# A hybrid decoder layer on one core: three sums of weights and one difference of token operands go from VectorE to GpSimd, and one token tile is scaled by itself

## The reference

```
h    = rms_norm(x, g_pre)                       # x: 512 x 2048
proj = h @ w_in                                 # q, k, v, gate of each group; forget gates
A: 6 heads, MoBA block-sparse causal attention, T5 relative bias
B: 6 heads, forgetting attention: log_sigmoid(fb + b_forget), cumulative sum as bias
C: 4 heads, attention into rms_norm(mem, g_mem) @ w_mem_kv   # mem: 256 x 2048
y    = concat(out_group * silu(gate))
x    = x + rms_norm(y @ w_out, g_post)
```

## Time and profile before

| | |
|---|---|
| median of 3 runs | 887.97 us (887.89 to 888.15) |
| profiled execution, whole | 889.66 us |
| its span | 887.9 us |
| TensorE busy | 865.6 us, 97% |
| VectorE busy | 727.2 us, 82% |
| ScalarE busy | 536.8 us, 60% |
| GpSimd busy | 75.9 us, 9% |
| mean granted TensorE clock | 0.994 of full |

### The profile page before, as it was taken

The page is one execution under the profiler, slowest core; times in us unless marked ns, Lnnn a source line. Parts: engine busy times, 40 slices in busy tenths (PEclk is TensorE's granted clock), DMA queues, the critical chain, the costliest instruction groups (busy, mean ns, idle before and its releaser), DMA issues.

```text
span 887.9 us, 13757 instructions
## 1 busy us (share of the span) xinstructions
PE 865.6 (97%) x5181; PEld 766.0 (86%) x5181; DVE 727.2 (82%) x1025; ACT 536.8 (60%) x918; POOL 75.9 (9%) x84
## 2 busy tenths in 40 slices
PE   9998999999999999999999999999999989999995
PEld 6997999988888888888888888888888878778884
DVE  5799789988888888888888888888888886975558
ACT  6795556565656565656565656565656575654452
POOL 0000310000000000000030303030301000000000
PEclk9999999999999999999999999999999999999999
DMA  9980586567668577657677768577644597466845
GB/s 289 303 200 23 165 181 165 148 172 159 160 171 196 137 178 176 161 163 177 153 183 170 165 171 185 144 185 170 161 121 107 172 366 259 146 214 208 289 190 189
DMA packets 179143, 161.37 MB, mean 182 GB/s; under 512 B 7353, under 2 KB 144217, under 8 KB 177670
## 3 DMA queue, kind: packets, MB, share of 16 engines
q1 hardware_dynamic: 170166, 142.66, 52.6%
q0 software_dynamic: 8704, 16.78, 13.7%
q10 hardware_dynamic: 208, 1.07, 0.4%
HBM read 152.33 MB, written 43.28 MB: 220 GB/s over the span
## 4 chain that ended last, share of the span: by engine, by line
PE 78%; DVE 12%; ACT 6%; issue 4%; DVEq 0%; POOL 0%; ACTq 0%; POOLq 0%
PE d_ps L709 19%; PE d_ps L714 10%; PE e_ps L709 10%; PE e_ps L714 5%; PE c_ps L709 5%; PE pt_ps L819 3%; DVE ring L1482 3%; PE d_ps L658 3%; PE c_ps L714 2%; PE d_ps L659 2%; PE d_ps L660 2%; ACT ring L1032 2%; PE score_ps L659 2%; PE score_ps L658 2%; PE score_ps L660 2%
## 5 line engine op out<-in xcount | busy, mean ns | idle before, releaser
L1482 DVE TENSOR_TENSOR ring<-raw,ring 128x1024 fp32r<-128x1024 f32 x134 | 164.5, 1230 | 48.6 <-ACT ring L1032 48.5
L1482 DVE TENSOR_TENSOR ring<-sums,ring 128x1024 fp32r<-128x1024 f32 x112 | 137.5, 1227 | 51.2 <-ACT ring L1032 51.1
L1032 ACT ACTIVATE ring<-raw 128x1024 fp32r<-128x1024 f32 x134 | 140.7, 1055 | 41.5 <-PE d_ps L660 15.4
L709 PE MATMUL d_ps<-late,ring 128*128 128x512 f32 x576 | 145.1, 394 | 0.0
L1032 ACT ACTIVATE ring<-sums 128x1024 fp32r<-128x1024 f32 x112 | 118.1, 1054 | 16.3 <-DVE sums L1509 13.1
L709 PEld LDWEIGHTS d_ps<-late,ring 128*128 128x128 f32 x576 | 103.4, 189 | 18.5
L714 PEld LDWEIGHTS d_ps<-late,ring 128*128 128x128 f32 x576 | 78.6, 190 | 5.7
L714 PE MATMUL d_ps<-late,ring 128*128 128x256 f32 x576 | 80.2, 282 | 0.0
L1509 DVE TENSOR_TENSOR sums<-raw 128x1024 f32<-128x1024 f32 x56 | 68.7, 1227 | 0.1
L1509 DVE TENSOR_TENSOR sums<-sums,raw 128x1024 f32<-128x1024 f32 x56 | 68.5, 1223 | 0.0
L2057 POOL DMA_DIRECT2D sum_dram<-in_w_out_dram x32 | 28.8, 900 | 421.0 <-DMA sum_dram<-in_w_out_dram 275.2
(11 more groups left out here) (387 smaller groups left out, 1915.4 us busy)
## 6 DMA issues: line engine op xcount, KB each, us to landing
raw<-in_w_in_dram SPq DMA_DIRECT2D x112, 512.0 KB, 5.7
sum_dram<-in_w_out_dram POOLq DMA_DIRECT2D x32, 512.0 KB, 7.4
raw<-sum_dram SPq DMA_DIRECT2D x32, 512.0 KB, 3.9
raw<-in_w_out_dram SPq DMA_DIRECT2D x24, 512.0 KB, 7.3
raw<-in_w_mem_kv_dram SPq DMA_DIRECT2D x16, 512.0 KB, 7.9
sum_dram<-in_w_out_dram SPq DMA_DIRECT2D x16, 512.0 KB, 6.4
sum_dram<-sum_dram SPq DMA_DIRECT2D x16, 512.0 KB, 6.1
stage<-in_x_dram SPq DMA_DIRECT2D x4, 1024.0 KB, 10.8
```

What stands on the lines that cost most here:

```text
L709: pe.matmul(bank[:], w[:, 0, k], both[:, k], start=i in (TOK_A, TOK_B) and k == 0, stop=False, skip_group_check=True)
L1032: act.activation(dst, src, ACTF.Copy).then_inc(hi_done, 1)
L1482: return dve.tensor_tensor(dst, a_, hi_.bitcast(F32), ALU.subtract)
```

## The change

Three things change. The third token tile (tile 4) is scaled by itself, ahead of `lo_mem(10)`, in place of together with tile 5; ScalarE takes one root more. For the first pair, sums 0, 1 and 2 are made by GpSimd; sum 3 and all sums of the other pairs stay on VectorE. The difference for token operand G is made by GpSimd, between its second and third sum. Waits follow from that: the load into the slot of the first pair's R11 waits for `lo_operand(0, 0)` too, and `lo_late(TOK_C)` waits for the difference. The shapes are as before: 1024 columns on 128 partitions for a sum, 2048 for the difference.

```
-ROOTS = 4
+ROOTS = 5
...
                         sp.wait_ge(sum_done, 4 * p + (4 if j == R12 else 3))
+                        if p == 0 and j == R11:
+                            sp.wait_ge(lo_done, operand(0, TOK_A) + 1)
...
# ScalarE
             squares(4)
+            root(4, 4)
             hi_mem(8)
...
-            root(5, 4, 2)
+            root(5, 5)
...
# VectorE
                 s = SUM_OF[i]
+                if p == 0 and s < SUMS:
+                    return
...
-                    dve.wait_ge(sum_done, 4 * p + 2)
+                    dve.wait_ge(sum_done, 4 * p + (2 if p else SUMS))
...
             def lo_late(i):
                 dve.wait_ge(late_hi, LATE_ORDER.index(i) + 1)
+                if i == TOK_C:
+                    dve.wait_ge(late_f32, 1)
...
-            scale_tiles(2, 2)
+            scale_tile(2)
             lo_mem(7)
-            scale_tiles(3, 3)
+            scale_tile(3)
...
             take_keys(3)
+            scale_tile(4)
             lo_mem(10)
             lo_whole(TOK_A)
             lo_mem(11)
-            scale_tiles(4, 4, 2)
+            scale_tile(5)
...
             lo_operand(0, 0)
-            add_weights(0, 1)
             lo_v_mem(2)
             lo_late(TOK_B)
             lo_operand(0, 1)
             lo_v_mem(3)
-            add_weights(0, 2)
-            dve.wait_ge(parts_made, 5)
-            dve.tensor_tensor(token_f32(TOK_G), token_f32(TOK_G), token_f32(TOK_C), ALU.subtract).then_inc(late_f32, 1)
             lo_operand(0, 2)
             lo_late(TOK_C)
...
# GpSimd, behind the memset of wf and ahead of the wait for f_z
+            def add_first(s, one, two):
+
+                pool.tensor_tensor(sum_tile(0, s), one, two, ALU.add).then_inc(sum_done, 1)
+
+            pool.wait_ge(bank_turned, 4 * TILES)
+            for j in (R11, R21, R22):
+                m = piece(0, j)
+                pool.wait_ge(raw_landed[m % RAW], 16 * (m // RAW + 1))
+            add_first(0, raw_tile(piece(0, R21)), raw_tile(piece(0, R22)))
+            pool.wait_ge(sum_done, 1)
+            add_first(1, sum_tile(0, 0), raw_tile(piece(0, R11)))
+            pool.wait_ge(parts_made, 5)
+            pool.wait_ge(whole_ready, 2)
+            pool.tensor_tensor(token_f32(TOK_G), token_f32(TOK_G), token_f32(TOK_C), ALU.subtract).then_inc(late_f32, 1)
+            pool.wait_ge(sum_done, 2)
+            add_first(2, raw_tile(piece(0, R11)), raw_tile(piece(0, R21)))
```

More of the change, by code:

```diff
@@ L1536, in rstd, with scale_tile @@
                 chain(dve.tensor_tensor(stat[:, 4, c], stat[:, 2, c], stat[:, 3, c], ALU.mult))
[L1538 to L1544, removed]
+            def scale_tile(t):
+                dve.wait_ge(squares_done, t)
+                rstd(t, t)
+                one = stage[:, t % 4]
+                dve.tensor_scalar(one, one, stat[:, 4, t:t + 1], None, ALU.mult).then_inc(tile_scaled, 1)
             def lo_memory(b0, b1):
```

## The result

The changed kernel takes 893.05 us (median of 5 runs, 892.70 to 894.26), the kernel before 888.15 us on the same chip (5 runs, 887.89 to 889.35). The ratio is 1.0055, with a 95% interval of 1.004 to 1.007: slower by half a per cent. The profiled execution took 894.26 us, its span is 892.4 us, 4.5 us longer than that of before.

A forecast was written before the change was run, and what follows sets the result against it. TensorE bounds the kernel, its product C waiting for VectorE's queue. Holds of +9.6 against -4.46 put C's low half at 91.2 us, C +3.2 later: 887.97 + 3.2 = 891.2 us; range 884.5 to 893.8, likeliest case's own 889.8 to 893.

The forecast's parts named there:

- The scaling at 0: Scaling tile 4 by itself gains nothing: VectorE waits for ScalarE before 59.93 anyway; cost taken as 0.
- 4.46 us off the queue ahead of C: Two sums of 1.13 us and the 2.20 us difference leave VectorE before C's low half ends at 86.10.
- GpSimd holds VectorE for each column: From 63 to 84 us VectorE stands still while GpSimd reads SBUF, 2.1 ns a column.
- The holds' sum: Three GpSimd sums at 2.1 us and a difference at 4.3 hold VectorE 10.6 us, +9.6 after cover.
- Who wins each turn matters little: Order of GpSimd and VectorE matters little: one-SBUF operations of 0.33 us pitch give cover, one or two at a time.
- The clock: TensorE's clock before product C: +2.4 us if it holds, +4.1 if it falls before B; middle +3.2 taken.
- The half clock in C, 2.6 us: In the kernel before, product C's 24 matmuls at 1.2 GHz cost 2.6 us more than at full clock.
- Product C as the place that decides: Product C waits for VectorE's low half; TensorE is full behind it, so C's shift reaches the end nearly whole.
- The engines don't hinder each other: Rival, chance 0.25: GpSimd costs VectorE only 0.26 us an instruction; C starts at 83.2, clock holds, 882.3 us.
- The clock survives at a shorter hold: Rival, chance 0.17: 1.7 to 1.9 ns a column, product C at full clock, 888.5 to 889.5 us.
- The clock stays down through C: Rival, chance 0.08: TensorE's several stops keep C partly at half clock, or 2.6 ns a column; 893.5 to 895 us.
- Only the scaling counts: Rival without its own chance: GpSimd reads in VectorE's gaps, VectorE's queue comes out even, 888.0 us.

The follow-up runs named there:

- the writes: The changed kernel with GpSimd's three sums and difference replaced by fills that read nothing: 883.26 us, ratio 0.9936.
- the copies: The changed kernel with GpSimd copying one operand in place of each of its three sums and the difference: 886.57 us, ratio 0.9972.
- The twin: The changed kernel with tiles 4 and 5 scaled as a pair again, so only GpSimd's part of the change remains: 892.63 us, ratio 1.0040.
- the two runs that show an execution near 888.1: The kernel before with tile 4 scaled by itself, and the kernel before with two idle GpSimd fills of 1024 columns: ratios 0.9996 and 0.9993.
- the scaling alone: The kernel before with only tile 4's scaling changed, GpSimd's work left as it was: 888.45 us, ratio 0.9996.
- difference behind F: The changed kernel with GpSimd's difference for G made to wait until VectorE has written F's low half: 893.08 us, ratio 1.0046.
- the one that wrote C's low half first: The kernel before with ScalarE copying C, VectorE subtracting later, and C's low half written ahead of its product's weights: 887.11 us, ratio 0.9980.

## Why the prediction was right, and where it was not

Forecast 891.2 us, slower, by turns at about 2.1 ns a column; measured 893.05, slower, by that mechanism. It is inside the range, and just past the top of the likeliest case's own (889.8 to 893).

- **The scaling at 0.** Shown, by itself, at 0.9996.
- **4.46 us off the queue ahead of C.** Right: it is what closes the sum from 86.10 to 92.18, and with GpSimd's reads gone the queue really is shorter (C's low half ends at 82.07).
- **GpSimd holds VectorE for each column.** Right in kind: 2.17 ns for the first two sums, 2.16 for the difference, against 2.1 from the 512-column row. That it is the read, and no fee for an instruction, is shown by the writes and the copies. The Trainium skill (SBUF — State Buffer, "Who interferes with whom") has both sides of this: a VectorE instruction with two SBUF inputs contends with a GpSimd instruction that reads SBUF, not with one that only writes. Both sides agree here (4.43 us of hold for the difference, none for the memset in its place).
- **The holds' sum.** Forecast 10.6 less 1.0 of cover, +9.6; measured +10.4. The price makes 0.5 of the difference and the lost cover 0.3 (0.67 us where I had 1.0). The Trainium skill's GPSIMD Engine Reference ("3.1 Elementwise — side-by-side cycle accounting") has 4497 ns for an addition of 2048 columns, which as an estimate would have made the holds 11.2 us before cover; the row here is 4.60 us, the hold 4.43, the sum before cover 11.1. The page was nearer than my row.
- **"Who wins each turn matters little."** This is a step that failed. For VectorE's queue and for the time it holds (waiting for F's low half gave the same median). But I had laid out TensorE's stops from a turn that went the other way. The low half of F came last, so the long stop came before the forget gates, until 81.65, and not before product A; A began at 85.90, B at 90.48 where I had 87.9, and C at 93.36 where I had 91.3.
- **The clock.** I gave one fall, in the stop before B, as a possibility at 4.1 us and 2.4 without it, and took 3.2 between. It fell twice in the changed kernel's profile, the first time after a stop of 2.29 us, and most of product A ran at 1.2 GHz. The twin, whose A ran at full clock, has C at 91.87, in line with the queue; the changed kernel pays 1.1 us more. So of the profile's 4.5 us, 3.4 are the queue (predicted 2.4: the holds' 0.8 and the later start of 0.15 are the difference) and 1.1 the clock (predicted 0.8). The medians differ by 4.9, 0.4 more than the two profiles do.
- **The half clock in C, 2.6 us.** This term was mis-sized for most executions, and it went unnoticed. I read it from the one profile of before, a long execution (889.66), and then added the difference to the median (887.97). The row at 91.74 is already product D's, so even there it is 2.45; in the two runs that show an execution near 888.1 it is 1.5, and there the change has 1.0 us less of slow clock to win back. The twin (892.70) against the scaling alone (888.34), both profiled on one chip, shows it: C begins 5.97 us later (85.90 to 91.87), the 1.5 us are gone, and the mark moves by 4.5 (93.21 to 97.69). So it was partly luck that 3.2 came near: 1.0 us was missing here and 1.0 in the queue, and the 0.8 added for a fall ahead of C is not needed by the twin.
- **Product C as the place that decides.** Half right. In the twin, C waits for its low half to the end. In the changed kernel it is TensorE's own queue, slowed in A, that reaches C last.
- **The rivals.** *The engines don't hinder each other* would have given 882.3; the version that only writes, in which they don't, took 883.26, so the mechanism is ruled out and its price was well worked out. *The clock survives at a shorter hold* is ruled out by the hold. *The clock stays down through C* didn't come, the fall in A did. *Only the scaling counts* is ruled out.

Left open: after which stop the clock falls. Stops of 2.29, 2.28 and 2.01 us (after, difference behind F, one operand) came with a fall and 2.29 us in the twin did not; the 1.43 and the 0.74 us came with none. I can't tell more from these runs. I also can't say for certain which of the two patterns most executions of the changed kernel had, as only one was profiled. The spans of the other four, 890.9 to 891.3 us, are close to the twin's 890.9 and not to the profiled 892.4, so the slow product A is probably not the usual case.

## What to carry to other kernels

Moving an elementwise instruction with two SBUF operands from a full VectorE to GpSimd costs VectorE more than it saves: 2.2 us of standing still for a sum that takes VectorE 1.13. VectorE's instructions that read one operand from SBUF and the other from PSUM ran on beside it (0.67 us of cover here), and writes on GpSimd were free; a VectorE with gaps in that place was not tried. And before moving work to another engine, look at where the late operand stands in its own queue: of all the versions here that compute the whole layer, the one that wrote C's low half first did best.

## What was unexpected in the hardware

- The turns are strict and for whole instructions. A 48-column VectorE instruction of 0.20 us took 2.42 behind a 1024-column sum, and GpSimd's next sum, free by then, let two more VectorE instructions of together 0.32 us wait 2.22.
- A GpSimd addition costs more than twice a copy: 2.2 us against 1.04 for 1024 columns, and 4.4 against 1.90 for 2048. The copy of 2048 columns is no slower than VectorE's two-operand instruction of that size, 2.20 us.
- The same stop of 2.29 us, for the same cause at the same place, came with a fall of TensorE's granted clock to half in the changed kernel's profile and with none in its twin's.
